# A second mixer in a new order: slabs, fillers, remainders on VectorE, gates by tanh

## What is computed

```python
h = rms_norm(x, norm_mix_pre[layer])
proj = h @ w_in                      # 1024 x 8208
(cu, cb, cc, rq, rk, rv, rg, gq, gk, gv, gr, ga_down,
 gate_a, gate_b, gate_c) = split_columns(proj)
y_a = short_conv(cu, cb, cc, conv_w)             # width 3
rq, rk = rotary(rq), rotary(rk)
y_b = head_norm(retention(rq, rk, rv), ret_gn_w, center=True) * silu(rg)
log_a = log_sigmoid(ga_down @ gla_w_a2 + gla_b_a) / 16
y_c = head_norm(gated_linear_attention(gq, gk, gv, log_a), gla_gn_w, center=False) * silu(gr)
merged = (sigmoid(gate_a) * (y_a @ w_branch_a) + sigmoid(gate_b) * (y_b @ w_branch_b)
          + sigmoid(gate_c) * (y_c @ w_branch_c))
x = x + rms_norm(merged @ w_out, norm_mix_post[layer])
h = rms_norm(x, norm_ffn_pre[layer])
x = x + rms_norm((silu(h @ w_gate) * (h @ w_up)) @ w_down, norm_ffn_post[layer])
```

## Time and profile before

| | |
|---|---|
| median of three runs | 2738.68 us (2735.82 to 2748.15) |
| the profiled execution's own time | 2728.94 us |
| its span | 2727.1 us |
| mean granted TensorE clock | 0.916 |
| HBM traffic in the span | 229 GB/s |

### The profile page before, as it was taken

One profiled execution on the slowest core, in us unless ns is written; L12 is line 12 of the kernel. 1 busy time (PEld: TensorE's weight loads), 2 busy tenths in 40 slices (PEclk: granted clock), 3 DMA queues, 4 the chain that ended last, 5 costly groups with the idle time before them and its releaser, 6 DMA issues.

```text
span 2727.1 us, 31511 instructions
## 1 busy us (share of the span) xinstructions
PE 2350.6 (86%) x13190; PEld 1624.8 (60%) x13190; DVE 606.7 (22%) x1109; ACT 639.9 (23%) x857; POOL 649.8 (24%) x171
## 2 busy tenths in 40 slices
PE   4999977769989998997998697879899797797997
PEld 2468736643333333333333396877899687786997
DVE  1002123341111211111121251122222161132231
ACT  2101421121111111111111333421333433412332
POOL 2100000010000000000000275602577565311874
PEclk7996978969999999999999798979899799888998
DMA  9433360329999999999999577541344443330542
GB/s 271 87 126 121 106 233 31 130 105 427 428 428 427 428 428 428 428 427 429 425 428 428 180 148 161 131 149 62 112 154 153 155 156 124 139 140 31 186 163 85
DMA packets 138000, 626.93 MB, mean 230 GB/s; under 512 B 11276, under 2 KB 23180, under 8 KB 113036
## 3 DMA queue, kind: packets, MB, share of 16 engines
q1 hardware_dynamic: 132544, 622.06, 60.1%
q0 software_dynamic: 1056, 0.20, 0.6%
q10 hardware_dynamic: 4268, 2.68, 0.4%
HBM read 623.69 MB, written 1.05 MB: 229 GB/s over the span
## 4 chain that ended last, share of the span: by engine, by line
issue 72%; PE 13%; POOL 11%; DMA 1%; DVE 1%; ACT 1%; POOLq 0%; DVEq 0%; SPq 0%; ACTq 0%
POOL ring_rounded L2097 10%; PE bank L1550 5%; PE bank L1038 3%; PE bank L1565 2%; PE bank L1388 2%; DMA ring<-in_w_in 1%; POOL arenaA L2083 1%; PE bank L1397 0%; PE bank L1487 0%; DVE arenaA L1928 0%; PE bank L1479 0%; POOL arena_rounded L2090 0%; PE bank L1510 0%; DVE arenaA L1974 0%; PE bank L1235 0%
## 5 line engine op out<-in xcount | busy, mean ns | idle before, releaser
L2097 POOL TENSOR_TENSOR ring_rounded<-ring,ring_rounded 128x2048 fp32r<-128x2048 f32 (+2 forms) x148 | 612.9, 4169 | 1522.3 <-ACT ring_rounded L828 1522.3
L1288 PE MATMUL bank<-ring,arenaA 128*64 128x512 f32 x3072 | 693.0, 601 | 38.8 <-DMA ring<-in_w_lin 27.5
L1288 PEld LDWEIGHTS bank<-ring,arenaA 128*64 128x64 f32 x3072 | 211.2, 138 | 461.6 <-issue 390.4
L1038 PE MATMUL bank<-arenaA,ring 128*128 128x256 f32 (+1 forms) x1408 | 342.0, 405 | 21.2 <-ACT arenaA L659 9.2
L1388 PE MATMUL bank<-arena_rounded,ring_rounded 128*128 128x256 f32 x2688 | 342.9, 290 | 7.9 <-ACT arena_rounded L835 7.9
L1388 PEld LDWEIGHTS bank<-arena_rounded,ring_rounded 128*128 128x128 f32 x2688 | 337.9, 198 | 9.5 <-issue 8.5
L828 ACT ACTIVATE ring_rounded<-ring 128x2048 fp32r<-128x2048 f32 (+2 forms) x148 | 244.3, 1699 | 358.9 <-DMA ring<-in_w_in 101.5
L1038 PEld LDWEIGHTS bank<-arenaA,ring 128*128 128x128 f32 x1408 | 274.7, 196 | 90.3 <-issue 37.8
L1550 PE MATMUL bank<-arena_rounded,ring_rounded 128*128 128x256 f32 x2112 | 256.1, 284 | 8.0 <-ACT arena_rounded L941 8.0
L1550 PEld LDWEIGHTS bank<-arena_rounded,ring_rounded 128*128 128x128 f32 x2112 | 255.7, 193 | 8.6 <-issue 8.6
L1890 DVE TENSOR_SCALAR arenaA<-bank 128x512 f32<-128x512 f32 x32 | 22.1, 692 | 506.7 <-PE bank L1288 506.7
(11 more groups left out here) (337 smaller groups left out, 1878.0 us busy)
## 6 DMA issues: line engine op xcount, KB each, us to landing
ring<-in_w_gate SPq DMA_DIRECT2D x64, 2048.0 KB, 23.2
ring<-in_w_lin SPq DMA_DIRECT2D x64, 2048.0 KB, 25.6
ring<-in_w_down SPq DMA_DIRECT2D x64, 2048.0 KB, 21.5
ring<-in_w_in SPq DMA_DIRECT2D x39, 2048.0 KB, 11.5
ring<-in_w_ada SPq DMA_DIRECT2D x12, 2048.0 KB, 7.8
ring<-in_w_ffn_gate SPq DMA_DIRECT2D x10, 2048.0 KB, 8.4
ring<-in_w_ffn_up SPq DMA_DIRECT2D x10, 2048.0 KB, 7.7
ring<-in_w_ffn_down SPq DMA_DIRECT2D x12, 1536.0 KB, 6.4
```

The lines of the kernel that those rows point to most:

```text
L1038: last = pe.matmul(dst, w[:, c, base + m * P:base + (m + 1) * P], rhs(c), start=(c == 0), stop=(c == kc - 1))
L1288: last = pe.matmul(bank[b][k * SLOTS:(k + 1) * SLOTS, :], lhsT(c), slot(j)[:, c % 4, k * 512:(k + 1) * 512], start=False, stop=(c == DC - ...
L2097: pool.tensor_tensor(place2(name, ringR)[:, a:b, :], w[:, a:b, :], hi[:, a:b, :], ALU.subtract).then_inc(w_lo, 1)
```

## The change

- The slabs of the mixer come in a new order, rq and rk first. gq and gk become one slab of 512 columns, and ga leaves the ring: its 16 columns of both layers are loaded once (`gaRaw`), by two loads on ScalarE's queue behind the router's and bias loads, and rounded in place (gaH, gaL). The mixer has 16 split slabs in place of 18.
- TensorE's order: rq, rk, ga, cu_0, the rotations, cu_1, cb, cc, the logits, rv; then the retention heads with rg, gq, gv, gr as what is placed between the small steps; then the linear attention, each score and attend behind a gate group of its own; the second sums and rows between branch groups.
- VectorE computes all remainders wL (`rest(k)`), at fixed places of its list; GpSimd's loop over both layers is gone. The convolution comes after the logits.
- The gates are evicted as tanh(g/2) in place of sigmoid(g). The merge multiplies by 1 + t, and the eviction of the out projection by 0.5. Branch a is merged in place.
- SP's loop over the layers is written out, with fixed addresses.

The diff, cut to its core ("..." where lines are left out; the new functions `decay`, `gla_head`, `gla_scores`, `decayed` and `masked` hold the former loop bodies):

```diff
--- before.py
+++ after.py
+        gaRaw = at(18960, 2, DC * GR)
+        gaH, gaL = at(19216, DC, GR, buf=arenaR), at(19344, DC, GR, buf=arenaR)
...
-            ("cu", 512), ("cb", 512), ("cc", 512), ("rq", 512), ("rk", 512), ("rv", 512), ("rg", 512), ("gq", 256),
-            ("gk", 256), ("gv", 512), ("gr", 512), ("ga", 16), ("ga0", 512), ("ga1", 512), ("gb0", 512), ("gb1", 512),
-            ("gc0", 512), ("gc1", 512))]
+            ("rq", 512), ("rk", 512), ("cu", 512), ("cb", 512), ("cc", 512), ("rv", 512), ("rg", 512), ("gq", 512), ("gv", 512),
+            ("gr", 512), ("ga0", 512), ("ga1", 512), ("gb0", 512), ("gb1", 512), ("gc0", 512), ("gc1", 512))]
...
+        for n in ("rq", "rk", "ga", "cu", "cb", "cc", "rv", "rg", "gq", "gv", "gr"):
+            groups2 += [("act", n, f"{n}_{i}") for i in range(1 if n == "ga" else 2)]
...
-            with sp.Fori(0, 2) as L:
+            for L in range(2):
...
+            moe_loads += [(gaRaw[:, L, :].rearrange("p (c n) -> p c n", c=DC),
+                           A["w_in_2"][L][:, C2["ga"]:C2["ga"] + GR].rearrange("(c p) n -> p c n", p=P)) for L in range(2)]
...
+                act.activation(gaH, gaRaw[:, bass.DynSlice(L, 1), :].rearrange("p l (c n) -> p (l c) n", c=DC), ACT.Copy).then_inc(m_hi, 1)
...
+                def feats(name, buf, ahead=None, func=ACT.Copy):
+                    empty(f"{name}_0", buf[:, 0:2, :], func, src=two)
+                    if ahead is not None:
+                        rounded(ahead)
+                    empty(f"{name}_1", buf[:, 2:4, :], func, src=two)
+                feats("rq", retQ, 2)
+                feats("rk", retK, 3)
                 empty("ga_0", glaA[0:GR, :], src=lambda b: b[0:GR, 0:T])
-                rounded(13)
+                feats("cu", convU, 4)
+                feats("cb", convB, 5)
+                feats("cc", convC, 6)
+                empty("rv_0", retV[:, 0, :])
+                rounded(7)
                 act.wait_ge(c_abs, L + 1)
                 act.activation(lln, lab, ACT.Exp, scale=-1.0).then_inc(c_ln, 1)
                 act.wait_ge(c_ln, L * 2 + 1)
                 act.activation(lln, lln, ACT.Ln, bias=1.0).then_inc(c_ln, 1)
+                empty("rv_1", retV[:, 1, :])
+                fillers = [lambda: empty("rg_0", retG[:, 0:2, :], ACT.Silu, src=two),
+                           lambda: empty("rg_1", retG[:, 2:4, :], ACT.Silu, src=two),
+                           lambda: empty("gq_0", glaQ, scale=GD ** -0.5, src=two), lambda: empty("gq_1", glaK, src=two),
+                           lambda: empty("gv_0", glaV[:, 0, :]), lambda: empty("gv_1", glaV[:, 1, :]),
+                           lambda: empty("gr_0", glaR[:, 0:2, :], ACT.Silu, src=two),
+                           lambda: empty("gr_1", glaR[:, 2:4, :], ACT.Silu, src=two)]
+                for h in range(RH):
+                    fillers[2 * h]()
+                    act.wait_ge(r_o, L * 8 + (h + 1))
+                    act.activation(headY[:, h, :], bank[6][:, 0:T], ACT.Copy).then_inc(r_oc, 1)
+                    rounded(8 + h)
+                    fillers[2 * h + 1]()
+                    act.wait_ge(r_c, L * 4 + (h + 1))
+                    act.activation(headY[:, h, :], bank[7][:, 0:T], ACT.Copy)
+                    act.activation(headSq[:, h, :], bank[7][:, 0:T], ACT.Square).then_inc(r_cc, 1)
...
+                    empty(f"gate{x}_{i}", gates[x][:, 2 * i:2 * i + 2, :], ACT.Tanh, scale=0.5, src=two)
...
+                gate_group(0)
                 act.wait_ge(h_ms, L * 2 + 1)
                 act.activation(hcol, hcol, ACT.Sqrt).then_inc(h_root, 1)
...
+                rounded(12)
+                gate_group(1)
+                decay(0)
+                decay(1)
+                gate_group(2)
+                rounded(13)
+                decay(2)
+                gate_group(3)
+                decay(3)
+                gate_group(4)
+                rounded(14)
+                decay(4)
+                gate_group(5)
+                decay(5)
+                gate_group(6)
+                gla_head(0)
+                rounded(15)
+                decay(6)
+                gate_group(7)
+                gla_head(1)
+                decay(7)
+                gate_group(8)
+                gate_group(9)
+                gate_group(10)
+                gla_head(2)
+                gate_group(11)
+                gla_head(3)
...
+                    empty(f"out_{i}", mixC[:, 2 * i:2 * i + 2, :], scale=0.5, src=two)
...
+                for nm in ("rq", "rk"):
                     for i in range(2):
                         mix2(nm, f"{nm}_{i}", i)
-                rows2("rv", "rv_0", 0)
+                b = open2("ga_0")
+                for part, (w, h) in enumerate(((gaH, hH), (gaH, hL), (gaL, hH))):
+                    if part == 2:
+                        pe.wait_ge(m_lo, L * 3 + 3)
+                    for c in range(DC):
+                        last = pe.matmul(b[0:GR, 0:T], w[:, c, :], h[:, c, :], start=(part == 0 and c == 0),
+                                         stop=(part == 2 and c == DC - 1))
+                last.then_inc(c_lin, 1)
+                mix2("cu", "cu_0", 0)
...
+                mix2("cu", "cu_1", 1)
+                for nm in ("cb", "cc"):
+                    for i in range(2):
+                        mix2(nm, f"{nm}_{i}", i)
...
+                for t in range(2):
+                    rows2("rv", f"rv_{t}", t)
+                fillers = [lambda i=i: mix2("rg", f"rg_{i}", i) for i in range(2)]
+                fillers += [lambda i=i: mix2("gq", f"gq_{i}", i) for i in range(2)]
+                fillers += [lambda t=t: rows2("gv", f"gv_{t}", t) for t in range(2)]
+                fillers += [lambda i=i: mix2("gr", f"gr_{i}", i) for i in range(2)]
...
                 for h in range(RH):
-                    gate_group(2 * h)
+                    fillers[2 * h]()
                     if h + 1 < RH:
                         ret_scores(h + 1)
                     pe.wait_ge(r_p, L * 4 + (h + 1))
-                    if h >= 1:
-                        pe.wait_ge(r_oc, L * 8 + h)
+                    pe.wait_ge(r_oc, L * 8 + h) if h else pe.wait_ge(*emptied2(G2["rv_1"], L))
                     attend(retV, h, retP[:, h % 2, :])
-                    gate_group(2 * h + 1)
+                    fillers[2 * h + 1]()
...
+                gate_group(0)
                 pe.wait_ge(r_cc, L * 4 + 4)
                 head_sums(0)
+                gate_group(1)
                 head_rows(0)
...
+                gate_group(2)
+                for k in range(4):
+                    gla_scores(k)
+                    gate_group(3 + k)
+                gla_attend(0)
+                gla_scores(4)
+                gate_group(7)
+                gla_attend(1)
+                for k in range(3):
+                    gla_scores(5 + k)
+                    gate_group(8 + k)
+                gla_attend(2)
+                gate_group(11)
+                gla_attend(3)
+                branch2("a", yA, 0)
                 pe.wait_ge(r_oc, L * 8 + 8)
                 head_sums(1)
+                branch2("a", yA, 1)
+                branch2("a", yA, 2)
                 head_rows(1)
+                branch2("a", yA, 3)
+                for i in range(4):
+                    branch2("b", yB, i)
                 pe.wait_ge(h_y, L * 2 + 2)
-                for x, y in (("a", yA), ("b", yB), ("c", yC)):
-                    w = slab2(f"br{x}")
-                    for i in range(4):
-                        pair2(w, f"br{x}_{i}", i, lambda c, y=y: y[:, c, :], 4)
+                for i in range(4):
+                    branch2("c", yC, i)
...
+                def rest(k):
+                    name = SPLIT[k]
+                    w, hi = place2(name), place2(name + "_hi", ringR).bitcast(F32)
+                    n = w.shape[1]
+                    for h, (a, b) in enumerate(((0, n // 2), (n // 2, n))):
+                        dve.wait_ge(w_hi, L * (2 * NSPLIT) + (2 * k + h + 1))
+                        dve.tensor_tensor(place2(name, ringR)[:, a:b, :], w[:, a:b, :], hi[:, a:b, :], ALU.subtract).then_inc(w_lo, 1)
+                rest(0)
...
+                rest(1)
+                rest(2)
+                rest(3)
...
+                rest(6)
...
+                    rest(7 + h)
+                rest(11)
...
+                head_ms(0)
+                head_col(0)
+                heads(0, yB, V2("ret_gn_w_2"), retG)
+                decayed(0)
+                decayed(1)
+                rest(12)
+                decayed(2)
+                rest(13)
+                decayed(3)
+                masked(0)
+                decayed(4)
+                rest(14)
+                decayed(5)
+                decayed(6)
+                rest(15)
+                decayed(7)
+                masked(1)
...
+                def merge(x, g_, i):
+                    name = f"br{x}_{i}"
+                    dve.wait_ge(*made2(name, L))
```

(31 more changed lines are left out.)

233 lines of the change are left out of this document (74 added, 159 removed).

## The result

The changed kernel takes 2628.08 us, the median of four runs (2614.46 to 2633.16), against 2739.01 for the kernel before beside it (four runs, 2735.82 to 2748.15). The ratio is 0.9594, 95% interval 0.9567 to 0.9622: 4.1% faster. The profiled execution took 2633.16 us with a span of 2631.3, 95.8 us less than the one of before. In the changed one L1402 is the group of 48 (before L1388), L1052 the plain matmul, L830 the rounding, L844 the eviction, L1976 VectorE's remainder.

What follows compares the result with a forecast made beforehand. TensorE was taken as the bound, gains coming from its idle and low-clock time in the mixers. -57.0 - 54.2 - 3.6 + 11.6 = -103.2 took the median 2738.7 to 2635 us; own range 2605 to 2660, full range 2603 to 2680.

Steps and rivals of the forecast that it cites:

- Mixers, -57.0 and -54.2: Mixers of layers 0 and 1: TensorE at full clock with few holes takes 260.8 us, saving 57.0 and 54.2 us.
- 2.5 us in hand before the decays: Linear attention: a group of 5.72 us precedes each decay's score, leaving about 2.5 us in hand; table loads priced at 0.
- Remainders on VectorE: Mixer and feed-forward: 4.6 us a slab, 140 us more VectorE work per layer; GpSimd's holds go, feed-forward cost 0.
- Two loads on ScalarE's queue, +11.6: First block: two issues, 2.44 and 11.14 us, delay ScalarE's evictions from 540.35 to 551.9, +11.6 us; bounds 0 to 20.3.
- Start of layer 1, -3.6: Start of layer 1: first slab's load comes earlier, squares end 4.6 us sooner, VectorE's first remainder costs 1, net -3.6.
- Half the gain lost to order: Rival, chance 0.14: late loads hold ScalarE's and VectorE's in-order work, evictions and banks; gives -52, 2687 us.
- tables: Rival, chance 0.10: tanh and exp change tables on ScalarE, 2 x 17.9 us more, 2671 us at most.
- slow subtraction: Rival, chance 0.07: VectorE's subtraction as slow as GpSimd's, 9.2 us a slab, 12 us a layer, 2659 us.
- nothing: Rival, chance 0.04: TensorE's holes stay and only move, -10 to +10 us of 2739.
- hole (a): Mixer: convolution and remainder after ScalarE's rounding of slab 6 come late for rg_0, TensorE waits 1.7 us.
- (b): Mixer: exp and ln behind the rounding of slab 7 make the first mask late, TensorE waits 2.7 us.
- the rival on loads: Rival, chance 0.03: loads become the bound, slower than before; landings up to 19.2 us cost nothing, at 30 it gives 2750.

Runs made afterwards that it cites:

- Experiment 5: Changed kernel with the linear attention's four scores in a row again, gate groups moved ahead and between the attends: 2661.90 us, ratio 0.9747 to the kernel before.
- experiment 4: Changed kernel with its gates evicted by sigmoid again in place of tanh: 2632.21 us, ratio 0.9635 to the kernel before.
- Experiment 2: Changed kernel with the weights' remainders subtracted by GpSimd again, in the former loop: 2665.5 us, ratio 0.9766 to the kernel before.
- Experiment 6: Changed kernel with ScalarE's and VectorE's loops over the two layers written out: 2625.87 us, ratio 0.9603 to the kernel before.

## Why the prediction was right, point by point

- **Mixers, -57.0 and -54.2: right, -58.7 and -55.9**, by the mechanism given. TensorE's work at full clock and the holes made 260.8, measured 259.1. The busy part was forecast at 254.8 and is 256.0 and 254.9; the idle part at 6.0 and is 3.1 and 4.2, as each layer has only one of the two holes. The row matmuls take 1.83 us for 15 of 16 (forecast 1.8); a slab's remainder is 4.5 us (forecast 4.6). Experiment 5 undoes one interleaving and gets its wait back.
- **Slack.** 2.5 us in hand before the decays was about right: with up to two more table loads of 1.28 in front of each, TensorE waits 1.4 us for them in all (experiment 4). The feed-forward stayed at 192.7 and 192.9 us with the remainder on VectorE.
- **Remainders on VectorE: the right sign, and too small a part in the text.** The sum took the holds of VectorE as one item among the holes. Experiment 2 shows that without this part 37 us of the gain are lost. The cost on VectorE, 140 us a layer, is 147. The new order packs VectorE's serial steps close behind roundings, and so needs GpSimd silent more than the old one did.
- **Two loads on ScalarE's queue, +11.6: mis-sized, +3.5.** The step "one issue like the router's and one like its follower" failed: the 10.73 us stay with the load of `b_router` and do not pass on to what stands behind. It was within the bounds given (0 to 20.3), at the cheap end. One thing was left out: the rounding behind the loads waits 0.85 us for them, and what it releases on GpSimd holds VectorE's addition, 1.0 us on the path. The sign "ScalarE's first block-one eviction near 552" seems met, with 554.7, but by luck: 13.3 us of that are the clock, and against the out projection's start the eviction is 3.0 us later than before, not 11.6 or more.
- **Start of layer 1, -3.6: wrong, +0.9.** The step "ScalarE rounds the first slab at 2131.5, since SP issued it at 2116.9" took the load for the limit. In the changed kernel the slab was issued 8.6 us ahead of ScalarE's evictions of the feed-forward's end, and not beside them, and the rounding did not follow. Experiment 6 shows the loop's jump as what ended last; without it the rest of the step comes out, the squares 4.6 us earlier and the whole 3.8. In the kernel before ScalarE's row at that place carries "7.49 <-issue" too, and not "<-DMA": it had been there to read.
- **Carrying it over to the median.** 13.3 us of the profiled difference were the first block's clock in that execution. The forecast's -103.2 stands between the -95.9 of the profiles and the -109 without that shift, beside -110.9, -99.5 and -108.7 by medians of three sets of runs. That the sum comes so near is luck in part: it priced the two loads 8.1 us too dear and the mixers 3.4 too long, the start of layer 1 4.5 and the rest 1.0 too short, which leaves 6. The medians of the kernel before alone differ by 10 to 13 us between the first set (2739.0) and the later ones. The forecast's own range, 2605 to 2660, is not the sum of its parts (2601 to 2648); nothing else rests on it.
- **Rivals.** Half the gain lost to order, tables, slow subtraction, nothing: none came at its price. The sign of the first one, ScalarE's waits for loads in front of TensorE's waits, did appear, as the walk with its late roundings had it: ScalarE's longest wait for a slab, 6.34 us, is the one ahead of hole (a), and 3.82 us stand ahead of (b). They cost 1.4 and 2.6 us, and so the 19.2 us of landing that "cost nothing" in the rival on loads are too many. How near the bound is was not tried.
